# Expert weights loaded in TensorE's order, and the pair matrix built by comparing spread places

## The reference, cut to what matters

```python
lg = xt @ w_rg + b_rg                      # 4 groups, top 1
le = xt @ w_re + b_re                      # 8 experts in the group, top 2
comb = g_w * oh_g * softmax(top2(le_sel))  # weight of each (token, expert)
for g in range(4):                         # 8 experts of each group
    h = silu(xt @ w_gate[g]) * (xt @ w_up[g])
    y = y + (h * comb) @ w_down[g]
x2 = LN2(alpha * x1 + y)
```

## Time and profile before

| | |
|---|---|
| median of 3 runs | 592.07 us (590.85 to 595.0) |
| profiled execution | 588.4 us, with a span of 586.7 us from the first to the last instruction |
| PE busy | 535.3 us, 91% of the span |
| DVE, ACT, POOL busy | 291.4, 193.1 and 58.7 us |
| moved by DMA | 151.88 MB, mean 259 GB/s |
| mean granted TensorE clock | 0.976 |

### The profile page before, as it was taken

How to read it: one execution, slowest core, us unless ns; L and a number is a source line. 1 busy time by engine, 2 the same in 40 slices (tenths; PEclk the granted TensorE clock), 3 DMA queues, 4 the chain that set the end, 5 groups by cost and what they waited for, 6 DMA issues and landing times.

```text
span 586.7 us, 9606 instructions
## 1 busy us (share of the span) xinstructions
PE 535.3 (91%) x3664; PEld 385.7 (66%) x3664; DVE 291.4 (50%) x621; ACT 193.1 (33%) x363; POOL 58.7 (10%) x86
## 2 busy tenths in 40 slices
PE   7899879999999979998999999998888899959992
PEld 7899768888999978766654444544444444446771
DVE  3443786555574865686722222222222222259976
ACT  4434444443462360163241111111111121345433
POOL 2000003322443420000000000000000000000121
PEclk9999999999999989969999999999999999979997
DMA  8996336865323940195739999999999999950001
GB/s 280 368 349 201 110 117 204 261 200 163 133 84 101 323 170 2 58 424 234 280 139 426 420 422 424 420 422 421 423 423 421 422 421 419 366 210 1 1 37 54
DMA packets 47565, 151.88 MB, mean 259 GB/s; under 512 B 3105, under 2 KB 27878, under 8 KB 35105
## 3 DMA queue, kind: packets, MB, share of 16 engines
q1 hardware_dynamic: 42754, 136.93, 60.4%
q0 software_dynamic: 3728, 12.08, 6.6%
q10 hardware_dynamic: 1046, 2.37, 1.2%
HBM read 148.59 MB, written 2.90 MB: 258 GB/s over the span
## 4 chain that ended last, share of the span: by engine, by line
PE 65%; DMA 14%; DVE 11%; ACT 3%; issue 3%; SPq 2%; POOL 1%; DVEq 0%; POOLq 0%; ACTq 0%
PE bank L1813 15%; PE bank L1494 15%; DMA ring<-in_w_up_dram 11%; PE bank L1454 8%; PE bank L1826 7%; PE bank L1682 5%; DMA ring<-in_w_in_dram 3%; PE bank L1835 2%; PE bank L1912 2%; PE bank L1760 2%; PE bank L1549 1%; ACT arena L630 1%; DVE gw_low L1320 1%; PE bank L1819 1%; PE bank L1563 1%
## 5 line engine op out<-in xcount | busy, mean ns | idle before, releaser
L1813 PE MATMUL bank<-ring,arena 128*64 128x256 f32 x1024 | 128.8, 392 | 10.6 <-DMA ring<-in_w_up_dram 7.3
L1813 PEld LDWEIGHTS bank<-ring,arena 128*64 128x64 f32 x1024 | 71.0, 134 | 66.6 <-issue 27.2
L1243 DVE TENSOR_TENSOR arena<-bank,arena 128x512 f32 x32 | 22.1, 692 | 143.7 <-PE bank L1835 143.7
L1494 PE MATMUL bank<-x_high,w_high 128*128 128x320 f32 x248 | 79.0, 319 | 2.1 <-ACT arena L592 2.1
L1494 PE MATMUL bank<-x_low,w_high 128*128 128x320 f32 x248 | 76.7, 309 | 0.0
L1494 PE MATMUL bank<-x_high,w_low 128*128 128x320 f32 x248 | 76.5, 308 | 0.0
L1826 PE MATMUL bank<-ring,arena 128*64 128x512 f32 x256 | 61.9, 604 | 0.0
L895 DVE TENSOR_TENSOR w_low<-ring,w_high 128x1024 fp32r<-128x1024 f32 x32 | 40.1, 1260 | 27.3 <-ACT w_high L574 27.2
L1494 PEld LDWEIGHTS bank<-x_high,w_high 128*128 128x128 f32 x248 | 46.6, 188 | 3.7 <-issue 3.6
L1494 PEld LDWEIGHTS bank<-x_low,w_high 128*128 128x128 f32 x248 | 46.7, 188 | 0.1
L1494 PEld LDWEIGHTS bank<-x_high,w_low 128*128 128x128 f32 x248 | 46.6, 188 | 0.0
(11 more groups left out here) (303 smaller groups left out, 884.0 us busy)
## 6 DMA issues: line engine op xcount, KB each, us to landing
ring<-in_w_gate_dram SPq DMA_DIRECT2D x32, 1024.0 KB, 18.1
ring<-in_w_up_dram SPq DMA_DIRECT2D x32, 1024.0 KB, 20.1
ring<-in_w_down_dram SPq DMA_DIRECT2D x32, 1024.0 KB, 16.8
ring<-in_w_in_dram SPq DMA_DIRECT2D x16, 1024.0 KB, 11.0
arena<-in_cache_k_dram POOLq DMA_DIRECT2D x16, 256.0 KB, 3.7
arena<-in_cache_v_dram POOLq DMA_DIRECT2D x16, 256.0 KB, 3.8
ring<-in_w_o_dram SPq DMA_DIRECT2D x4, 1024.0 KB, 10.7
ring<-in_w_ple_gate_dram SPq DMA_DIRECT2D x4, 1024.0 KB, 15.6
```

The source lines that it names most:

```text
L1243: V.tensor_tensor(YsT[:, :, bass.ds(place, WIN)].rearrange("p (d c) n -> p c d n", d=2), b[:, :].rearrange("p (c d n) -> p c d n", c=4, d= ...
L1494: last = mm(bank[j % 2][:, 0:T], w[:, j % 4, k, :], x[:, k, :], start=(k == n == 0), stop=(k == KD - 1 and n == 2))
L1813: last = mm(b[WIN * f:WIN * (f + 1), 0:256].rearrange("p (s n) -> p s n", s=2), x[:, WIN * k:WIN * (k + 1)], w[:, :, k, f, :], start=(k == ...
```

## The change

Two things are changed. SP issues the expert weights in another order: gate and up of expert n+1 come ahead of down of expert n. And `Pj` is no longer turned out of `PT`. Instead PE spreads `pos1` and `pos2` over the rows of two banks (`spread_places`, six transposes in the midst of expert 29), and DVE compares them with the row's number in five turns of two instructions (`pairs`). Inside expert 3 PE now does `down(2)` ahead of the spreading of the weights and of `turn_result(1)`.

```diff
-            for e in range(4):
-                for r, (w, k) in enumerate(((wg_d, KD), (wu_d, KD), (wd_d, 2))):
-                    load(U_EXPERT + 3 * e + r, w[e], k)
...
+            load_pair(0)
+            for e in range(1, 5):
+                load_pair(e)
+                load_down(e - 1)
             with sp.Fori(0, EARLY // 4 - 1) as i:
                 for j in range(4):
-                    for r, (w, k) in enumerate(((wg_d, KD), (wu_d, KD), (wd_d, 2))):
-                        slot = 3 * j + r
-                        sp.wait_ge(main["gu"] if r < 2 else main["y"], i * 4 + (j + 1))
...
+                    sp.wait_ge(main["gu"], i * 4 + (j + 2))
+                    load_again(3 * ((j + 1) % 4), wg_d, KD, i * 4 + (j + 5))
+                    load_again(3 * ((j + 1) % 4) + 1, wu_d, KD, i * 4 + (j + 5))
+                    sp.wait_ge(main["y"], i * 4 + (j + 1))
+                    load_again(3 * j + 2, wd_d, 2, i * 4 + (j + 4))
...
# ACT
-                    pairs_out()
+                    weights_out()
+                    act.wait_ge(main["yt"], 1)
                 result_out(main, n)
...
# DVE
                         dve.wait_ge(weight_set, 2)
+                        dve.wait_ge(ga_ps, 2 * KD)
...
+            def pairs(n):
+
+                if n == 0:
+                    dve.wait_ge(rank_ps, 3)
+                number = cst[:, C_PAIR + n:C_PAIR + n + 1]
+                link(V.tensor_scalar(Pj[:, n, :], bank[6][:, 0:T], number, None, ALU.is_equal))
+                V.scalar_tensor_tensor(Pj[:, n, :], bank[7][:, 0:T], number, Pj[:, n, :].bitcast(F32), ALU.is_equal, ALU.add).then_inc(pj_set, 1)
...
                     put(main, first + (j - 1), bank[4 + (j + 1) % 2], before)
+                    if pairs_too and j > 0:
+                        pairs(j - 1)
...
             crowded = dve.value_load(flag[0:1, 0:1], min_val=0, max_val=1)
+            pairs(3)
+            pairs(4)
             for n in range(2):
                 low_gate(n)
             put(main, EXPERTS, bank[4 + 1], last_place)
...
# PE
-            def turn_pairs():
+            def spread_weights():
 
                 pe.wait_ge(ga_out, 16)
...
+                pe.wait_ge(ct_set, 1)
+                for hf in range(2):
+                    mm(bank[6 + hf][:, 0:320], ones[:, :], CT[:, 320 * hf:320 * (hf + 1)], start=True, stop=True).then_inc(ct_set, 1)
+
+            def spread_places():
+
+                pe.wait_ge(pe_out, 6)
+                for b, pos in ((bank[6], pos1), (bank[7], pos2)):
                     for t in range(TILES):
                         r = ROWS[t]
...
+                        last = nc.tensor.transpose(b[:, P * t:P * t + r], pos[0:r, t:t + 1].to_broadcast([r, P]), ident[0:r, 0:r])
+                last.then_inc(rank_ps, 1)
...
+                    if places_too and j == 0:
+                        spread_places()
                     if behind[j] == 3:
                         other_half()
-                        turn_pairs()
+                        pe.wait_ge(main["ys"], 1)
+                        here(j - 1, 2)
+                        down(main, first + (j - 1), slots[3 * j - 1])
+                        spread_weights()
+                        turn_result(main, first + (j - 2), bank[4 + j % 2])
+                        continue
...
             def combine(n, t):
 
+                pe.wait_ge(pj_set, n + 1)
```

More of the change, by code:

```diff
@@ L79 @@
 C_ROW = C_IOTA + 32
-C_END = C_ROW + 2
+C_PAIR = C_ROW + 2
+C_END = C_PAIR + 5
 def constant_tables():
@@ L426, in _, with load_pair, load_down, load_again @@
             sp.dma_start(w_ple, a["w_ple"].rearrange("l (k p) d -> p (l k) d", p=P)).then_inc(cst_here, 16)
-            for e in range(4):
-                for r, (w, k) in enumerate(((wg_d, KD), (wu_d, KD), (wd_d, 2))):
-                    load(U_EXPERT + 3 * e + r, w[e], k)
+            def load_pair(e):
+                load(U_EXPERT + 3 * e, wg_d[e], KD)
+                load(U_EXPERT + 3 * e + 1, wu_d[e], KD)
+            def load_down(e):
+                load(U_EXPERT + 3 * e + 2, wd_d[e], 2)
+            def load_again(slot, w, k, expert):
+                src = w[bass.ds(expert, 1), :, :, :].rearrange("o p k n -> p (o k) n")
+                sp.dma_start(unit(slot, k), src).then_inc(w_in_slot[slot], 16)
+            load_pair(0)
+            for e in range(1, 5):
+                load_pair(e)
+                load_down(e - 1)
             with sp.Fori(0, EARLY // 4 - 1) as i:
                 for j in range(4):
-                    for r, (w, k) in enumerate(((wg_d, KD), (wu_d, KD), (wd_d, 2))):
-                        slot = 3 * j + r
-                        sp.wait_ge(main["gu"] if r < 2 else main["y"], i * 4 + (j + 1))
[L436 to L440, removed]
+                    sp.wait_ge(main["gu"], i * 4 + (j + 2))
[3 more added lines that the diff above has]
+                    load_again(3 * j + 2, wd_d, 2, i * 4 + (j + 4))
+            for e in range(EARLY + 1, EXPERTS):
+                load_pair(e)
+                load_down(e - 1)
+            load_down(EXPERTS - 1)
             for c in range(4):
@@ L782, in four_experts, with weights_out @@
                     result_out(main, first + (j - 1))
[L784 to L792, removed]
+            def weights_out():
+                for hf in range(2):
+                    act.wait_ge(ct_set, 2 + hf)
+                    nc.scalar.copy(slot_weight[:, 320 * hf:320 * (hf + 1)], bank[6 + hf][:, 0:320]).then_inc(weight_set, 1)
             gate_sigmoid(main, 1, bank[0])
@@ L1831, in turn_result @@
                 if isinstance(n, int) and n == 1:
[L1832 removed]
+                    pe.wait_ge(ga_out, 16)
                 pe.wait_ge(q["ys"], n)
@@ L1836, in turn_result, with four_experts @@
                 last.then_inc(q["yt"], 1)
-            def four_experts(first, slots, here, behind=(2, 2, 2, 2)):
+            def four_experts(first, slots, here, behind=(2, 2, 2, 2), places_too=False):
                 for j in range(4):
@@ L1873, in _ @@
             crowded = pe.value_load(flag[0:1, 0:1], min_val=0, max_val=1)
-            four_experts(EARLY + 1, [(U_LATE + n) % RING for n in range(11)] + [(U_LATE - 1) % RING], late)
+            four_experts(EARLY + 1, [(U_LATE + n) % RING for n in range(11)] + [(U_LATE - 1) % RING], late, places_too=True)
             turn_hidden(main, EXPERTS)
```

16 lines of the change are left out of this document (4 added, 12 removed).

## The result

| | before | after |
|---|---|---|
| median of 4 runs | 591.46 us (587.75 to 595.0) | 581.83 us (580.76 to 583.63) |
| profiled execution | 588.4 us, span 586.7 | 580.9 us, span 579.2 |
| mean granted TensorE clock | 0.976 | 0.974 |

The change makes the kernel faster, by less than 2%: the ratio is 0.9857, with a 95% interval of 0.9812 to 0.9903, about 8.4 us. The two profiled executions differ by 7.5 us in their spans.

The account below looks back on a forecast made before the run. The prediction took the stream of expert weight loads to bound the first 28 experts, PE those behind. Its terms -9.9 + 0.9 + 0.5 made -8.5 us: 583.5 us as a median, range 580.5 to 588.0.

Parts of the forecast that it names:

- The stream bounds, and its last restart decides: Weight loads set the first 28 experts; PE's savings count only through the earlier issue at the stream's last restart.
- rival 2: Expert loads: the holes stay, only the new order gains one piece of 2.49 us; -1.1, 591.0 us; chance 0.08.
- Its size, -9.9: Landings of w_up 9.9 us earlier: 7.5 by three more pieces through at the last restart, 2.49 by the order.
- Piece 21: Gate of expert 8, the load at the stream's last restart, waiting for `gate_up(4)`; forecast issued at 304.3.
- 301.4, half a microsecond early: `put(1)` and `hidden(3)` on DVE behind `turn_result(1)` done at 301.4, before PE needs them in `gate_up(4)` at 302.
- until 305: Nine loads going out from 281.06 on take 22.4 us, so the stream is busy until 305.
- The six transposes, +0.9: On PE behind `gate_up(29)`, where PE bounds again: +0.9 us, bounds 0 and 1.2.
- The comparisons, 1.1 a pair: DVE's pairs of comparisons from PSUM in the last experts: 1.1 us each, 0.89 to 1.5.
- The end, +0.5: PE's last steps: `moe_done` comes 3.8 us later, PE's jump hides all but 0.5; range +0.5 to +3.
- Rival 1: Around `gate_up(4)`: late pair weights hold `put(1)` and `hidden(3)`, the stream restarts late; 4.1 us lost, 587.7 us; chance 0.13.
- Rival 3: PE's loop of experts: instructions are fetched again at each pass; +28 - 8.5, 611 us; chance 0.05.
- Rival 4: End of the experts: DVE's last pairs cost 1.5 us or more, the jump is short; about 586.5 us; chance 0.06.

Follow-up runs that it names:

- order_only: The kernel before with SP's new order of loads alone, PE, ACT and DVE as before; ratio 0.9937 to the kernel before.
- the straight kernels: PE's part of the branch for crowded experts left out of the kernel before (ratio 0.9945) and of the changed kernel (0.9843), both against the kernel before.
- places_only: The changed kernel with SP's old order of loads (gate, up, down of each expert); ratio 0.9952 to the kernel before.

## Why the prediction was right, step by step

- **The stream bounds, and its last restart decides: right.** order_only gave 5.80 where the theory had 5.8 and "only the order" 2.5 (rival 2). Beside the order, the time is won in the first 46 us behind `gate_up(1)` alone.
- **Its size, -9.9: too much by 1 to 2 us.** `gate_up(28)` came 7.9 earlier in the two profiles, and 8.9 between the means of six starts of this stream (186.98) and of two of before (195.84). Piece 21 went out 28.15 us behind `gate_up(1)` rather than 27.3, for two terms. The products of the weights were put at 0.9 us, but the earlier trace rows have 1.19 (298.37 to 299.56) and the trace after has 1.18; so `gate_up(4)` started 0.2 later (23.19 for 22.99 behind `gate_up(1)`). And "301.4, half a microsecond early" for `hidden(3)` took `put(1)` to stand right behind `turn_result(1)`; it started 1.0 us behind it, for the copy of the weights and the register load behind that, and `gate_up(4)` took 4.71 us rather than 4.14. The pieces ahead lasted as long as forecast: "until 305" is 28.0 behind `gate_up(1)`, and the 253 GB/s of the slice from 303 us on put the fall at some 27.9 (an estimate from that row). What is left to 7.9, about 1 us, was lost behind the restart. In the first profile that agrees with the 394 GB/s, for 425 before, in the 14 us there (1.0 us). In the second, 413 GB/s make only 0.4, so the cause stays open.
- **The match of 8.5 with 8.4 is in part luck.** 8.4 was timed, 2.7 either way; the two traces show 6.6 from `gate_up(1)` on, and 0.9 of the spans' difference lies ahead of it. The terms as measured add up to -6.4 with the 7.9 of the two profiles and to -7.4 with the 8.9 of the means. The runs don't decide between these and 8.5.
- **The six transposes, +0.9: 1.12**, near the upper bound, the rate of the old ones.
- **The comparisons, 1.1 a pair: 1.05. The end, +0.5: 0.39.** `moe_done` came 2.83 later and not 3.8: three pairs end where `low_gate` begins (507.38), but part of that time DVE had stood idle before, waiting for ACT. That the jump hides this was a guess from one row of issue; the straight kernels show it.
- **Rival 1** happened with a tenth of its price (0.45 of 4.1). **Rival 2** fell with order_only. **Rival 3** did not come about: between 340 and 480 us two packets of instructions moved, one on each of two queues, as in the kernel before (of which the earlier trace rows show one), and the last 134 us of the table of stretches, which hold most of the loop, run at the stream's 422 GB/s. **Rival 4** was 1.0 us away: by so much `moe_done` was ahead of PE's restart.

On the rule that stood beside rival 3, the Trainium skill ("Runtime: NRT & Kernel Launch", Instruction fetch mechanics) has a taken branch wait for a fetch where its target lies outside what is at hand. The jump at the end agrees: 5.89 us with the long block and a packet of instructions, none with the short one.

## What to carry to other kernels

Where a stream of weights bounds, ask which wait of the issuing queue ends its last pause: time saved on the compute engine counts only if it moves that issue, and two waits that cover each other must both go. Extra work belongs into the stretch that the stream bounds, not into the last steps behind it, where each microsecond shows unless a stall happens to cover it. A seldom used block that a jump passes over should be short: here its five copies cost 3.4 us at PE's restart, which also hid other work.

## What the runs showed that was not expected

- A jump over five unrolled windows took 6.2 to 6.6 us in the profiles (5.2 in places_only, where PE then waits for `moe_done`); over one window in a loop it took 0.23.
- The lead ahead of the experts varies by 5.5 us between profiled runs (`gate_up(1)` at 276.13 to 281.64), more than most steps told apart here.
- One issue of a transfer on SP can take 1.33 us rather than 0.33 (up of expert 8 at 304.75). What makes it long stayed open.
